# Six of thirteen row buffers given up in a gather-fed expert stage

## What is computed

```
q = (xb @ w_query)                       # 8 heads, two halves each
s_top, i_top = top_k(q . sub_keys, 16)   # per head and half
best, pos = top_k(all 16 x 16 sums, 16)  # 16 experts per head
g = softmax(best)
u = expert_u[eidx];  h = gelu(u . xb)    # 128 tokens x 8 heads x 16 experts
vv = expert_v[eidx]
out = sum over the 128 experts of g * h * vv
```

## Time and profile before

| | |
|---|---|
| median of 3 runs | 3213.3 us (3212.12 to 3214.76) |
| span of the profiled execution | 3210.9 us |
| first gather issued to last sum | 1816.2 to 3206.0 us |
| DVE, PE, ACT, POOL busy over the span | 49%, 79%, 33%, 18% |
| HBM read | 1051.6 MB, half of it the gathers |

### The profile page before, as it was taken

The page is one execution under the profiler, slowest core; times in us unless marked ns, Lnnn a source line. Parts: engine busy times, 40 slices in busy tenths (PEclk is TensorE's granted clock), DMA queues, the critical chain, the costliest instruction groups (busy, mean ns, idle before and its releaser), DMA issues.

```text
span 3210.9 us, 43682 instructions
## 1 busy us (share of the span) xinstructions
PE 2530.9 (79%) x17242; PEld 1248.3 (39%) x17242; DVE 1564.1 (49%) x3391; ACT 1048.7 (33%) x2457; POOL 581.5 (18%) x535
## 2 busy tenths in 40 slices
PE   8999988797988878878879878897778655555655
PEld 6677774484322222222228634343324211111111
DVE  4655655763100100100107466678675777777764
ACT  2533443521000000000006354577344444343433
POOL 0000000000000000000000143344443444444442
PEclk9999998998999999999999989898888777788778
DMA  4211302249999999999995499999999999999997
GB/s 152 101 58 66 122 26 112 92 158 382 427 427 427 427 427 427 427 427 427 427 411 195 176 418 399 417 418 383 420 419 420 420 420 419 420 419 420 420 419 331
DMA packets 128670, 1067.80 MB, mean 333 GB/s; under 512 B 14289, under 2 KB 17233, under 8 KB 27601
## 3 DMA queue, kind: packets, MB, share of 16 engines
q0 software_dynamic: 75456, 543.20, 41.0%
q1 hardware_dynamic: 53008, 521.81, 39.4%
HBM read 1051.58 MB, written 13.37 MB: 332 GB/s over the span
## 4 chain that ended last, share of the span: by engine, by line
DMA 50%; PE 34%; DVE 7%; ACT 6%; issue 2%; POOL 1%; ACTq 0%; DVEq 0%; SPq 0%; POOLq 0%
PE ps L92 33%; DMA gb<-in_peer_uv,eidx 27%; DMA gw<-in_eu 14%; DMA gw<-in_ed 8%; DVE gb L146 2%; PE ps L97 2%; ACT L168 1%; ACT dots L168 1%; ACT diag L168 1%; ACT prob L168 1%; POOL gb L86 1%; DVE prob L146 0%; DVE w_lo L115 0%; ACT prob_t L168 0%; DVE prob L120 0%
## 5 line engine op out<-in xcount | busy, mean ns | idle before, releaser
L92 PE MATMUL ps<-gb,diag 64*64 64x512 f32 x4096 | 662.0, 759 | 410.3 <-ACT diag L168 396.8
L146 DVE CUSTOM_DVE_ANT_0 gb<-gb,xn 128x1024 f32<-128x1024 f32 x512 | 627.1, 1225 | 378.5 <-DMA gb<-in_peer_uv,eidx 378.0
L86 POOL DMA_INDIRECT gb<-in_peer_uv,eidx x512 | 570.3, 1114 | 1312.6 <-PE ps L92 718.5
L92 PEld LDWEIGHTS ps<-gb,diag 64*64 64x64 f32 x4096 | 148.2, 155 | 847.6 <-ACT diag L168 746.3
L168 ACT ACTIVATE dots<-dots 128x1 f32<-128x1 f32 (+1 forms) x382 | 77.6, 203 | 618.3 <-DVE dots L146 611.5
L115 DVE TENSOR_TENSOR expert_act<-expert_act,ps 128x512 f32<-128x512 f32 x32 | 22.0, 687 | 523.8 <-PE ps L92 523.2
L92 PE MATMUL ps<-ga,xt 128*64 128x512 f32 x1024 | 229.2, 596 | 41.3 <-DMA ga<-in_eu 32.6
L92 PE MATMUL ps<-gw,xt 128*64 128x512 f32 x992 | 224.3, 601 | 25.4 <-DMA gw<-in_eu 16.2
L168 ACT ACTIVATE diag<-cons,dots 128x128 f32<-128x128 f32 x512 | 205.5, 401 | 41.1 <-ACT dots L168 0.4
L115 DVE TENSOR_TENSOR x<-x,ps 128x512 f32<-128x512 f32 (+1 forms) x96 | 61.4, 643 | 296.5 <-PE ps L92 294.9
L168 ACT ACT_TABLE_LOAD x124 | 159.1, 1283 | 8.1 <-PEq L3241 0.7
(11 more groups left out here) (360 smaller groups left out, 3616.9 us busy)
## 6 DMA issues: line engine op xcount, KB each, us to landing
ga<-in_eu SPq DMA_DIRECT2D x47, 2048.0 KB, 35.5
gw<-in_eg SPq DMA_DIRECT2D x46, 2048.0 KB, 30.7
ring<-in_wt SPq DMA_DIRECT2D x75, 1024.0 KB, 6.0
gw<-in_ed SPq DMA_DIRECT2D x32, 2048.0 KB, 35.5
ga<-in_ed SPq DMA_DIRECT2D x32, 2048.0 KB, 36.1
ga<-in_eg SPq DMA_DIRECT2D x17, 2048.0 KB, 32.2
gw<-in_eu SPq DMA_DIRECT2D x16, 2048.0 KB, 35.5
p_scratch<-spill SPq DMA_DIRECT2D x35, 256.0 KB, 2.1
```

The costliest lines, as they stand in the source:

```text
L86: self.e.indirect_dma_start(out, None, table, bass.IndirectOffsetOnAxis(ap=idx, axis=0)).then_inc(s, 16)
L92: i = self.e.matmul(out, l, r, start=st, stop=sp, skip_group_check=True)
L146: self.done(self.e.tensor_tensor_reduce(out=o, in0=a, in1=b, scale=scale, scalar=start, op0=o0, op1=o1, accum_out=acc), name)
```

## The change

The sixth early buffer (`gb5`), the three of `MIDDLE` and two of the three of `LATE` are dropped. Left are gb0 to gb4 and gb9 from the start, six buffers, and gb12 from row 244, seven. Nothing else in the program is edited; the waits and buffer addresses of all rows follow from the list.

```diff
-    EARLY = [M(f"gb{i}", 29744 + 2048 * i, 2048) for i in range(5)] + [M("gb5", 2048, 2048)]
-    MIDDLE = [M(f"gb{6 + i}", o, 2048) for i, o in enumerate((10240, 12288, 16384))]
+    EARLY = [M(f"gb{i}", 29744 + 2048 * i, 2048) for i in range(5)]
     THIRD = T("gb9", O_RING, 2048)
-    LATE = [T(f"gb{10 + i}", O_RING + 2048 * (NS - 1 - i), 2048) for i in range(2)] + [M("gb12", 18432, 2048)]
+    LATE = [M("gb12", 18432, 2048)]
     ROW_BUFFERS = [(t, 0, None) for t in EARLY[2:]] + [(THIRD, 0, ("used", 10)), (EARLY[0], 0, ("used", 13)), (EARLY[1], 0, ("used", 14))]
-    ROW_BUFFERS += [(t, 172, ("used", TILES + P0 - 1)) for t in MIDDLE]
     ROW_BUFFERS += [(t, GROW, ("used", 2 * TILES - 1)) for t in LATE]
```

## The result

The changed kernel takes 3237.3 us in the median of 4 runs (3236.3 to 3239.5), against 3213.7 us of before in 4 runs of its own: a ratio of 1.0073, 95% interval 1.0059 to 1.0087. That is 23.6 us slower, where 20 us were forecast.

A forecast was written before the change was run, and what follows sets the result against it. DMA was taken as the bound while rows are gathered. Late rows and pairs summed to 14.7 us at the lower floor, 24.8 at 7.5 us; the middle, 20 us, on 3213.3 gave 3233 us, range 3218 to 3262.

The forecast's parts named there:

- What bounds the kernel: While expert rows are gathered, DMA is the bound; fewer buffers cost time only where its queue runs dry.
- The floor: Time from a gather's issue to its dot with an empty queue: 6.37 to 7.55 us, ends 5.5 and 8.44.
- about 7 us: Sum of late-row delays if the skill's 4.4 us per 1 MB gather held, instead of 14.6 us.
- Rows 0 to 171: Early rows with one buffer less: 8.2 us lost at the 6.37 us floor, each stall capped at 2.5 us.
- The list of places: Rows named as late behind long PE matmul blocks: up to row 171, rows 21, 46 (2.5 us each), 89 (1.95), 136 (1.22).
- Rows 172 to 243: Rows with four buffers less: 6.5 us lost, at rows 209 (3.13), 221 (1.84), 233 (0.71) and 239 (0.79).
- The pairs: Rows 244 to 503, seven buffers for thirteen: about 3 us left over per round, cost 0 to 2.4 us.
- The total: Middle of 14.7 and 24.8 us, 20 us slower, so 3233 us; 10 to 45 us more had chance 0.75.
- A: Rival: weight tiles use the DMA during stalls and hide the cut; 3213 to 3218 us; chance 0.14.
- B: Rival: the buffer loop becomes the bound, gathers taking 10 us under a shallow queue; 3301 us; chance 0.08.
- C: Rival: weight tiles land sooner beside fewer queued rows, PE starts blocks sooner; faster, 3199 us; chance 0.03.

The follow-up runs named there:

- e3: Kernel before, with seven buffers instead of thirteen for the rows in pairs from row 244 on; 3215.5 us, ratio 1.0002.
- e2: Changed kernel with the three MIDDLE buffers brought back (six early, nine from row 172, ten from row 244); 3231.6 us, ratio 1.0044.
- e5: Changed kernel with each query projection's 32 PE matmuls cut into two events of 16, rows or choosing steps between; 3226.8 us, ratio 1.0041.
- e12: The changed kernel, unaltered, timed again later against before; 3237.0 us, ratio 1.0064.
- e1: Kernel before without MIDDLE and two of LATE: seven buffers to row 243, eight after; 3213.5 us, ratio 0.9998.
- e9: Kernel before with five buffers from row 244 on and those rows one by one, not in pairs; 3240.0 us, ratio 1.0074.
- e6: Kernel before, all its buffers kept, with each query projection's 32 matmuls cut into two halves; 3212.9 us, ratio 0.9996.
- e10: Kernel before with all thirteen buffers, but rows from 244 on one by one, not in pairs; 3214.5 us, ratio 0.9998.
- e11: Changed kernel with six buffers throughout, query projections split in halves and rows single, not in pairs; 3227.9 us, ratio 1.0040.
- e8: Kernel before, with six buffers instead of thirteen for the rows in pairs from row 244 on; 3226.6 us, ratio 1.0036.

## Why the prediction was right, and where it was off

*What bounds the kernel.* Right. The early rows could not spare one of their seven buffers, the rows in pairs could spare six of thirteen (e3), and where a buffer too many was gone it cost DMA idle time: DVE's wait for gathers grew by about what the kernel lost.

*The floor.* Right at its lower value: rows 46 and 221 took 6.37 and 6.46 us; rows 209, 29 and 21 stood at 7.25, 7.55 and 8.03. The shortest landings are 5.3 to 6.0 us over the fourteen profiles. The estimate from the Trainium skill's sum of 2.0 us and the bytes at 436 GB/s (DMA: Bandwidth & Descriptors, Anatomy of one DMA), 4.4 us for 1 MB, stays below every one of them. The prediction's "about 7 us" for that figure is also off: the same working with 4.4 us leaves rows 21, 46 and 209 with 1.8, 2.5 and 1.2 us, 5.5 in all.

*Rows 0 to 171.* The term was 8.2 us at a floor of 6.4 and, the same working done again, 11.5 at 7.5; it measured 15.9. The list of places was right but not complete. By the dots' times against before, counted from row 0's issue, row 21 cost 2.4 us, rows 42 to 52 around row 46 cost 2.7, row 89 1.6, and row 136 with those just ahead of it 2.7, more than the 1.22 of the list. Rows 29 to 35 cost 3.0 us that the list doesn't have. Row 23's dot came 6.0 us later than in before (1893.0 to 1899.0, by the timelines), but its sum 8.1 us later (1902.0 to 1910.1). It stood behind the same 32 matmuls in both; PE was slower. Before, then the changed kernel, row 22's eight matmuls and the block of 32 (the third number from the end is the granted clock as a share of 2.4 GHz):
```profile
1892.81:1893.83 1.02, 1.02 (x9) 0.21 (x9) 0.82 (x1) 0.00 (x0) 0.00 (x0) 1.00 0.97 410
1893.83:1901.00 7.17, 7.17 (x40) 6.06 (x39) 6.89 (x18) 4.32 (x12) 0.94 (x1) 1.00 1.01 424
...
1898.83:1900.74 1.91, 1.91 (x8) 0.30 (x8) 1.60 (x3) 0.41 (x2) 0.73 (x1) 0.50 1.01 425
1900.74:1909.06 8.32, 8.32 (x40) 6.89 (x38) 7.68 (x21) 5.08 (x14) 1.29 (x1) 0.86 1.01 422
```
The same matmuls took 1.91 us at 0.50 (1.2 GHz) for 1.02 us at 1.00, and the block 8.32 us at 0.86 for 7.17 us at 1.00. In the changed kernel PE had sat idle for 3.16 us ahead of row 21's matmuls, waiting for a diagonal; the clock was 1.00 in the matmuls before this gap and 0.50 in those right behind it. A working on a fixed trace keeps PE's times as they were. How much of the early loss is such slower work isn't shown.

*Rows 172 to 243.* 6.5 us forecast at a floor of 6.4 (11.0 at 7.5), 5.9 measured. e2 (nine buffers) and e5 (shorter blocks) each take it away whole, so both the count and the blocks are shown as its cause. Row by row the fit is poorer than the sum. Row 209, forecast at 3.13 us, cost 0.6, since a weight tile filled its stall; row 233, forecast at 0.71, cost 3.2, with the DMA at 112 GB/s; row 239 cost nothing; only row 221 came near, 2.1 for 1.84. That the sum came out is luck.

*The pairs.* 0 to 2.4 us forecast, -1.5 measured in the changed kernel and 0.8 (677.6 against 676.8) in e3, nothing that can be told from zero. Right, and with less to spare than it looked: six cost 12 us, five 138.

*The total.* 20 us from the middle of 14.7 and 24.8; 20.4 us of difference from the first issue on (25.0 in e12's profile), and 2.9 us ahead of it that no step of mine explains. The agreement is in part luck. At the middle the working gives 9.8, 8.8 and 1.2 us for the three stretches, and 15.9, 5.9 and -1.5 were measured: the first term was too small by about what the other two were too large.

*The rivals.* A (hidden) is out for the change as a whole, but its mechanism is real: at row 209 a weight tile did use the time. With one early buffer more nothing is lost (e1). B (the loop as the bound) is out for seven buffers in pairs. Below that the loop does become the bound, but not as B had it: what grew was the hold of a pair, 9.5 us for 7.1, while the gathers of e9, with five buffers, had a median landing of 8.2 us and not 10. C (tiles land sooner with fewer rows queued) is out: a tile's median landing is 9.0 us in e2, with six buffers in the early rows, and 9.1 in e1, with seven, as in before. That is how it would be by the Trainium skill's rule that each DMA engine takes turns between the rings that have work (DMA: Bandwidth & Descriptors, Queues, rings and completion order).
```profile
ring<-in_wt SPq DMA_DIRECT2D x27, 1024.0 KB, 9.0
```
```profile
ring<-in_wt SPq DMA_DIRECT2D x27, 1024.0 KB, 9.1
```

No version here beats before: its late stretch already runs at 420 GB/s, and e1, e3, e6 and e10 all end within 0.1% of it. What can be had is memory: e1 does the same time with eight buffers as before with thirteen.

## What to carry to other kernels

The number of buffers that a stream of transfers needs can be estimated as the time of one round (issue to use with an empty queue, plus the hold) over the time of one transfer. Which hold to take is the question. In the pairs the typical one (median, from dot to next issue, by the timeline of before) is 6.2 us, and (6.4 + 6.2) / 2.5 gives 5 buffers; the longest is that of row 256, from its dot below to the issue at 2568.17, 13.3 us, which gives 8.
```profile
2554.85 1.23 DVE L146 CUSTOM_DVE_ANT_0 gb<-gb,xn 128x1024 f32<-128x1024 f32 x1 [0.51 <-DMA gb<-in_peer_uv,eidx]
```
Measured, seven were enough, six cost 12 us, mostly at the two block ends with their long holds, and five cost 138 us. So the longest hold says from where on nothing is lost, and the typical one where every round starts to lose. For the longest, look for the in-order engine that frees the buffer and for the longest piece of other work in front of it. Beyond what is needed, more buffers only lengthened the queue here (26.4 us of landing against 11.3 at the same time). If memory is short, cutting the long piece in two (e5), or freeing rows singly and not in pairs (e11 against e8, 677.6 us for 688.8), can be worth as much as a buffer.

## What I had not expected

Seven buffers of 1 MB, with a landing of 11.3 us, move 418 GB/s from 2600 to 3100 us where thirteen move 420: depth beyond not running dry bought next to no rate. And the step from six to five buffers in the pairs is elevenfold in cost (12 to 138 us), with the rate falling from 409 to 345 GB/s in the stretch from 2600 to 3100 us.
